# First eight chunks of w_mod: six of them split into high and low halves, and the gates of x taken before those of the context

## The chip, the cores and the metric

The kernel runs on one core of a Trainium2 chip. The metric is the device time of one execution in microseconds (us). The engines are TensorE (PE, with its weight loads as PEld), VectorE (DVE), ScalarE (ACT), GpSimd (POOL) and SyncE (SP), which issues most of the transfers. Each engine works through its own instructions in order; they meet only at semaphores.

## What is computed

Two transformer blocks in float32, on 256 tokens of width 1024. The change concerns the opening of the first block: the modulation vectors, the normalised and modulated x and context, and the forget gates of both.

```python
mod = (silu(c) @ w_mod[l] + b_mod[l]).reshape(bsz, 6, 1024)      # w_mod: 1024 x 6144
mc = (silu(c_ctx) @ w_mod[l] + b_mod[l]).reshape(6, 1024)
hc = modulate(rmsnorm(ctx, g_mix[l]), mc[0], mc[1])              # h * (1 + scale) + shift
pc = hc @ w_in[l][:, :1536]                                      # f_f, f_b (512 each), i_c (512)
h = modulate(rmsnorm(x, g_mix[l]), mod[:, 0, None], mod[:, 1, None])
p = h @ w_in[l]                                                  # f_f, f_b, i_in, q, og, u, v, ga, gb
f = lb + (1 - lb) * sigmoid(f_logit)                             # forget_gate; log(f) and 1 - f are used
```

All that follows (two linear recurrences started from the context's final state, a gating unit, five feed-forward parts, two attentions) is untouched by the change.

## The kernel before

Weights come as pieces of 128 x 1024 in the order of a list (`weight_plan`), through ten slots. For each piece `split` on ScalarE makes the high part WH (L991, a copy rounded to fp32r) and `split` on VectorE the low part WL = RAW - WH (L1485). A product then is three fp32r products (high by high, high by low, low by high), 128 x 128 by 256 columns each. SyncE loads piece j when the group that used piece j - 10 is done (`used`). In `split_to("win", i)` both engines split up to five pieces ahead of chunk i of w_in, and a chunk is two pieces.

Ahead of the list stand eight chunks of w_mod, `FIRST = (4, 5, 6, 7, 0, 1, 2, 3)` (chunks 0 to 3 are the shift, 4 to 7 the scale), 1 MB each, which lie in the memory of slots 0 to 7. They are used unsplit: `mod_first(i)` on TensorE makes float32 products of SILC (silu of c and c_ctx, two columns) with MC[i] (L442). The result is a pair of rows; VectorE copies it (`mod_rows(i)`, L1529), TensorE turns it into columns with four small products (`mods_finish`, L433), and VectorE adds the bias to give MOD (L1519, in its own `mods_finish`, run at the head of the next `mod_rows`). Chunks from 8 on come through the list, split, and are multiplied in `mods` (L456, L457) with SILH, which has high and low parts of the two vectors as four columns.

For the norms, ScalarE squares x (XF) and the context (XC) in eight steps (`square`, L1011), VectorE (x, "nx") or GpSimd (context, "nc") adds them up (`gather`), TensorE sums over the partitions (`sums`, L409), ScalarE takes the root (L1017), VectorE the reciprocal (`invert`, L1505), TensorE spreads it over the partitions (`spread`, L398) and ScalarE copies it to RB (`rows_kept`, L1024). Only then `modulated` can run: for each of eight k steps VectorE makes TA (L1550), ScalarE adds the shift and rounds to HH or, for the context, HCH (L1030), and VectorE makes the low part HL or HCL (L1559).

The gates are chunks 0 to 3 of w_in, for x (source 0) and for the context (source 1): 48 products a chunk and source, sigmoid on ScalarE into FX or FC (L1066), then lb + (1 - lb) f on VectorE (L1622). The order on TensorE is written out: chunks 0 and 1 of x, chunks 0 and 1 of the context, then chunk 2 of each, then chunk 3 of each, all with `by_k_step`, which for each k waits for that step's HL or HCL alone. `pair` is the other routine: it waits for what it is given once (here the eighth low part), then runs tile by tile. Chunks 4 and 5 of w_in (values, VTX and VTC) follow for both sources, then the queries, and the state work that starts with Ln of FC (L1083). The order of VectorE and ScalarE is written out too: the context's `modulated` stands behind the last of x and ahead of all gates. `rows_in(0)` is a 512 KB transfer (GROW) issued from ScalarE's queue, first used with chunk 8 of w_mod.

Of the kernel before, what the change touches and what calls it, by code (L numbers as in the profile page):

```python
# [12 lines left out]
P = 128  # L13
# [109 lines left out]
def build(nc, a, out):  # L123
# [3 lines left out]
    with ctx:  # L127
        base = [nc.sbuf_base]

        def at_(name, shape, off, dt=F32):  # L130
            return nc.alloc_sbuf_tensor_at(name, shape, dt, offset=off)
# [63 lines left out]
        MR = Ring([at_(f"MR{i}", [4, T], tmp_at + 9216 + 1024 * i) for i in range(2)])  # L195
        ROW = ph("ROW", 72, [P, 3, 512])
# [76 lines left out]
        RINGS = (RT, RS, RB, SQ, ACC, TA, MR, BANK, QK, AB, LNB, SPB, AW, SW, SX, PT, MX, SL, GG, Y, XN, TN)  # L273
# [65 lines left out]
        def pe_program(pe, e):  # L339
# [79 lines left out]
            def mods_finish():  # L419

                while rows:
                    i = rows.pop(0)
                    b, empty = bank(("modt", i), ("mod", i))
                    pe.wait_ge(*at("mr", i))
                    pe.wait_ge(*empty)
                    nr = 4 if i >= 8 else 2
                    mr = MR.of(("mr", i))
                    if i // 4 in (2, 5):
                        m = e.matmul(b[:, 0:T], CST[0:nr, C_SEL:C_SEL + 1].to_broadcast([nr, P]), mr[0:nr, :],
                                     start=True, stop=True)  # L430
                    else:
                        for t in range(2):
                            m = e.matmul(b[:, 2 * t:2 * t + 2], mr[0:nr, t * P:(t + 1) * P],  # L433
                                         CST[0:nr, C_SEL:C_SEL + 2], start=True, stop=True)
                    m.then_inc(*sig("modt", i))

            def mod_first(i):
                b, empty = bank(("modp", i), ("mr", i))
                pe.wait_ge(s_mod[i], 16)
                pe.wait_ge(*empty)  # L440
                for k in range(KD):
                    m = e.matmul(b[0:2, 0:T], SILC[:, 2 * k:2 * k + 2], MC[i][:, k * 256:k * 256 + 256],  # L442
                                 start=(k == 0), stop=(k == KD - 1))
                m.then_inc(*sig("modp", i))
                mods_finish()
                rows.append(i)
# [20 lines left out]
            mod_first(5)  # L467
            mod_first(6)
            sums("nx")
            mod_first(7)  # L470
            spread("nx")
            mod_first(0)
            mod_first(1)
            sums("nc")
            mod_first(2)
            spread("nc")
            mod_first(3)
# [3 lines left out]
            for c0, n in ((0, 2), (2, 1), (3, 1)):  # L481
                for src, (xh, xl, low) in enumerate(((HH, HL, "hl"), (HCH, HCL, "hcl"))):
                    group = [("win", c0 + z, ("fg", src, c0 + z), ("fs", src, c0 + z)) for z in range(n)]
                    for k in range(KD):
                        by_k_step(k, group, xh, xl, at(low, k))
# [496 lines left out]
        def act_program(ac, e):  # L982
# [58 lines left out]
            rows_in(0)  # L1041
            for k in range(KD):
                square("nx", k, XF[:, k, :], (s_xf, 16))
            root("nx")
            rows_kept("nx", ("hl", 7))
            for k in range(KD):
                square("nc", k, XC[:, k, :], (s_ctx, 16))
            modulated("h", 0, 0, HH, 0, 2, lambda k: at("mod", 0))
            root("nc")
            modulated("h", 0, 0, HH, 2, 4, lambda k: at("mod", 1))  # L1050
            rows_kept("nc", ("hcl", 7))
            split(1)
            modulated("h", 0, 0, HH, 4, 6, lambda k: at("mod", 2))
            split(3)
            modulated("h", 0, 0, HH, 6, 8, lambda k: at("mod", 3))
            modulated("hc", 0, 1, HCH, 0, 8, lambda k: at("mod", 3))
            ac.wait_ge(*at("dve", "lb", 1))
            e.activation(LBV[:, 8:24], LBV[:, 8:24], ACT.Exp).then_inc(*sig("act", "lb e"))
            split(5)


            for c0, n in ((0, 2), (2, 1), (3, 1)):
                for src, dst in enumerate((FX, FC)):
                    for c in range(c0, c0 + n):
                        ac.wait_ge(*at("fg", src, c))
                        e.activation(dst[:, 2 * c:2 * c + 2, :], two(BANK.of(("fg", src, c))[:, :]),  # L1066
                                     ACT.Sigmoid).then_inc(*sig("fs", src, c))
                split_to("win", c0 + n - 1)
# [407 lines left out]
        def dve_program(dv, e):  # L1476
# [46 lines left out]
            def mod_rows(i):  # L1523
                mods_finish()
                nr = 4 if i >= 8 else 2
                mr, before = MR.take(("mr", i), ("modt", i))
                dv.wait_ge(*at("modp", i))
                dv.wait_ge(*after(before))
                e.tensor_copy(mr[0:nr, :], BANK.of(("modp", i))[0:nr, 0:T]).then_inc(*sig("mr", i))  # L1529
                rows.append(i)  # L1530
# [39 lines left out]
            mod_rows(4)  # L1570
            for k in range(1, 7):
                gather("nx", k)
            mod_rows(5)
            mod_rows(6)
            invert("nx")
            mod_rows(7)
            mod_rows(0)
            dv.wait_ge(*at("mod", 7))
            scale_of("va", 0, S_GMIX, 8, 0)
            mod_rows(1)  # L1580
# [3 lines left out]
            invert("nc")  # L1584
            mod_rows(2)
            modulated("h", XF, RB.of(("rb", "nx")), 0, 0, 0, HH, HL, 2, 4)
            split(1)
            mod_rows(3)
            modulated("h", XF, RB.of(("rb", "nx")), 0, 0, 0, HH, HL, 4, 6)
# [4 lines left out]
            dv.wait_ge(*at("rb", "nc"))  # L1594
            dv.wait_ge(*at("dve", "vc"))
            modulated("hc", XC, RB.of(("rb", "nc")), 8, 0, 1, HCH, HCL, 0, 8)
# [15 lines left out]
            split(5)  # L1612


            dv.wait_ge(*at("dve", "lb", 5))
            for c0, n in ((0, 2), (2, 1), (3, 1)):
                for src, dst in enumerate((FX, FC)):
                    for c in range(c0, c0 + n):
                        dv.wait_ge(*at("fs", src, c))
                        for t in range(2):  # L1620
                            i = 2 * c + t
                            e.tensor_scalar(dst[:, i, :], dst[:, i, :], OMLB(i), LB(i), ALU.mult,  # L1622
                                            ALU.add).then_inc(*sig("fm", src, i))
                split_to("win", c0 + n - 1)
# [576 lines left out]
        def sp_program(sp, e):  # L2201
            e.dma_start(SM[:, :], a["small"]).then_inc(s_const, 16)
            e.dma_start(CST[:, :], a["cst"]).then_inc(s_const, 16)
            for z, i in enumerate(FIRST):
                if z == 1:
                    e.dma_start(XF[:, :, :], a["xf"]).then_inc(s_xf, 16)
                if z == 4:
                    e.dma_start(XC[:, :, :], a["ctx"]).then_inc(s_ctx, 16)
                e.dma_start(MC[i][:, :], a["mod"][i]).then_inc(s_mod[i], 16)
            for j, (kind, i, cols) in enumerate(plan):  # L2210
                if j >= SLOTS:
                    sp.wait_ge(*at(*used[j - SLOTS]))
                elif j >= 2:
                    sp.wait_ge(*at("modp", FIRST[j - 2]))
# [117 lines left out]
```

## Time and profile before

| | |
|---|---|
| median of three runs | 1638.43 us (1636.14 to 1641.19) |
| profiled execution | 1636.97 us, span 1635.7 us |
| busy, share of the span | PE 94%, DVE 56%, ACT 48%, POOL 3% |
| mean granted clock of TensorE | 0.962 of 2.4 GHz |
| moved | 267.11 MB, mean 163 GB/s |

The profile shows one execution. "Busy" of TensorE counts matmuls, which overlap, so that a product of 0.28 us may follow the one before it after 0.12. In rows of single instructions the bracket at the end gives the engine's idle time before them and what ended it. The chain of waits is followed back from the last instruction, at each step to what released it.

### The profile page before, as it was taken

The numbers are of one execution on the slowest core, as the hardware profiler recorded it, in microseconds if no ns is written. First come the engines' busy times: TensorE is split into PE (matmuls) and PEld (weight loads), VectorE is DVE, ScalarE is ACT, GpSimd is POOL, SyncE is SP. The second block draws the span as 40 slices with busy tenths as digits, with TensorE's granted clock in tenths as the row PEclk, the third lists the DMA queues.
The fourth block names the chain that finished last, engine by engine and source line by source line (L and its number), as shares of the span: only waits on it lengthen the run. The fifth ranks groups of instructions, "written<-read, shape, count | busy, mean of one in ns | idle before, by whom it ended". The sixth has DMA issues, their size and how long they took to land.

```text
span 1635.7 us, 20070 instructions
## 1 busy us (share of the span) xinstructions
PE 1540.1 (94%) x8188; PEld 1277.9 (78%) x8188; DVE 917.1 (56%) x1294; ACT 792.2 (48%) x1153; POOL 47.8 (3%) x83
## 2 busy tenths in 40 slices
PE   7998999998999999999999999999999777899998
PEld 3897888886888878887898788878888675578886
DVE  2627664877555565555455655556554457365553
ACT  2525435554445355544565555455554444365542
POOL 1000200000000000000021000000000011000000
PEclk9999788999999999999999999999999888799999
DMA  9225353644565655555533455555555410145652
GB/s 380 79 81 204 128 194 129 232 145 163 182 187 186 201 164 186 185 191 180 168 128 126 155 184 184 193 180 179 185 188 190 146 54 26 37 155 183 188 185 103
DMA packets 72236, 267.11 MB, mean 163 GB/s; under 512 B 8016, under 2 KB 8272, under 8 KB 70736
## 3 DMA queue, kind: packets, MB, share of 16 engines
q1 hardware_dynamic: 69984, 258.87, 48.0%
q10 hardware_dynamic: 2160, 6.95, 1.2%
q8 instruction: 65, 1.06, 0.3%
q14 instruction: 27, 0.22, 0.0%
HBM read 264.74 MB, written 1.05 MB: 162 GB/s over the span
## 4 chain that ended last, share of the span: by engine, by line
PE 83%; DVE 8%; ACT 5%; issue 2%; DMA 1%; POOL 0%; ACTq 0%; SPq 0%; DVEq 0%
PE PS L691 20%; PE PS L707 12%; PE PS L709 12%; PE PS L708 12%; PE PS L342 4%; PE PS L343 4%; PE PS L344 4%; DVE WL L1485 2%; ACT WH L991 2%; PE PS L675 1%; PE PS L442 1%; PE PS L374 1%; PE PS L375 1%; PE PS L376 1%; PE PS L563 1%
## 5 line engine op out<-in xcount | busy, mean ns | idle before, releaser
L1485 DVE TENSOR_TENSOR WL<-RAW,WH 128x1024 fp32r<-128x1024 f32 (+1 forms) x472 | 569.9, 1224 | 361.7 <-ACT WH L991 361.2
L991 ACT ACTIVATE WH<-RAW 128x1024 fp32r<-128x1024 f32 (+1 forms) x472 | 484.4, 1053 | 290.6 <-DMA RAW<-in_up 169.9
L707 PE MATMUL PS<-WH,XH 128*128 128x512 f32 x912 | 376.7, 413 | 24.5 <-DVE WL L1485 14.4
L709 PE MATMUL PS<-WH,XL 128*128 128x512 f32 x912 | 357.9, 392 | 0.0
L708 PE MATMUL PS<-WL,XH 128*128 128x512 f32 x912 | 357.7, 392 | 0.0
L707 PEld LDWEIGHTS PS<-WH,XH 128*128 128x128 f32 x912 | 172.2, 189 | 77.3 <-DVE WL L1485 18.3
L709 PEld LDWEIGHTS PS<-WH,XL 128*128 128x128 f32 x912 | 172.0, 189 | 37.0
L708 PEld LDWEIGHTS PS<-WL,XH 128*128 128x128 f32 x912 | 172.6, 189 | 27.7
L691 PE MATMUL PS<-WH,GH 128*128 128x512 f32 x440 | 137.3, 393 | 0.0
L691 PE MATMUL PS<-WL,GH 128*128 128x512 f32 x440 | 135.6, 389 | 0.0
L691 PE MATMUL PS<-WH,GL 128*128 128x512 f32 x440 | 135.6, 389 | 0.0
L691 PEld LDWEIGHTS PS<-WH,GL 128*128 128x128 f32 x440 | 82.6, 188 | 17.4
L691 PEld LDWEIGHTS PS<-WL,GH 128*128 128x128 f32 x440 | 82.6, 188 | 17.4
L691 PEld LDWEIGHTS PS<-WH,GH 128*128 128x128 f32 x440 | 81.2, 188 | 17.2
L1958 DVE SCALAR_TENSOR_TENSOR GG<-PS,RP,SL 128x256 f32<-128x256 f32 x88 | 42.6, 484 | 88.7 <-ACT SL L1291 88.7
L1298 ACT ACTIVATE GH<-PS 128x256 fp32r<-128x256 f32 x110 | 42.2, 384 | 90.9 <-PE PS L675 90.8
L342 PE MATMUL PS<-HH,WH 128*128 128x256 f32 x224 | 66.0, 295 | 0.0
L343 PE MATMUL PS<-HL,WH 128*128 128x256 f32 x224 | 65.3, 292 | 0.0
L344 PE MATMUL PS<-HH,WL 128*128 128x256 f32 x224 | 65.2, 291 | 0.0
L675 PE MATMUL PS<-CST,GG 128*128 128x128 f32 x220 | 58.8, 271 | 0.0
L1291 ACT ACTIVATE SL<-PS,RP 128x256 f32<-128x256 f32 x88 | 41.7, 474 | 28.7 <-PE PS L709 28.7
L342 PEld LDWEIGHTS PS<-HH,WH 128*128 128x128 f32 x224 | 45.1, 201 | 0.9 <-issue 0.3
(365 smaller groups left out, 2133.8 us busy)
## 6 DMA issues: line engine op xcount, KB each, us to landing
RAW<-in_up SPq DMA_DIRECT2D x220, 512.0 KB, 4.7
RAW<-in_down SPq DMA_DIRECT2D x110, 512.0 KB, 3.2
RAW<-in_win SPq DMA_DIRECT2D x44, 512.0 KB, 5.4
RAW<-in_mod SPq DMA_DIRECT2D x32, 512.0 KB, 4.9
MC<-in_mod SPq DMA_DIRECT2D x8, 1024.0 KB, 16.8
RAW<-in_sbqk SPq DMA_DIRECT2D x16, 512.0 KB, 4.8
GROW<-in_grow ACTq DMA_DIRECT2D x9, 512.0 KB, 4.6
RAW<-in_wo SPq DMA_DIRECT2D x8, 512.0 KB, 3.7
```

The lines of the kernel that those rows point to most:

```text
L342: e.matmul(out_, lh, rh, start=first, stop=False)
L343: e.matmul(out_, lh, rl, start=False, stop=False)
L344: return e.matmul(out_, ll, rh, start=False, stop=last)
L675: m = e.transpose(o_[:, y * P:(y + 1) * P], gg[:, y * P:(y + 1) * P], IDN)
L691: m = e.matmul(b2[n][:, :], l, r[:, n * 512:(n + 1) * 512], start=(first and z == 0), stop=(last and z == 2), skip_group_check=True)
L707: e.matmul(o_[:, :], l, w[:, s], start=(k == 0), stop=False, skip_group_check=True)
L708: e.matmul(o_[:, :], l, wl[:, s], start=False, stop=False, skip_group_check=True)
L709: m = e.matmul(o_[:, :], ll, w[:, s], start=False, stop=(k == KD - 1), skip_group_check=True)
L991: e.activation(WH[s][:, 0:c], RAW[s][:, 0:c], ACT.Copy).then_inc(*sig("hi", j))
L1298: e.activation(GH[:, 2 * j:2 * j + 2, h * P:(h + 1) * P], two(BANK.of(("gt", v, j, h))[:, 0:T]), ACT.Copy).then_inc(*sig("gh", v, j, h))
L1485: e.tensor_tensor(WL[s][:, 0:c], RAW[s][:, 0:c], WH[s][:, 0:c].bitcast(F32), ALU.subtract).then_inc(*sig("lo", j))
L1958: m = e.scalar_tensor_tensor(gg[:, :], u, RP[:, v, h:h + 1], sl[:, :], ALU.mult, ALU.mult)
```

## The change

Six of the eight chunks (`SPLIT`; not 4 and 6) are split like the others: ScalarE writes the high part of a chunk in two halves into a ring of two buffers MH_, VectorE writes the low part over the chunk in place (ML_), and the new `mod_split(i)` on TensorE multiplies SILH with both, k step by k step, waiting for each half. A high buffer comes free when the products of the chunk that used it are done. x is loaded ahead of the chunks, the context behind four pieces of w_in, GROW after the context's squares. The sums of x stand after the first chunk. The gates of x are taken for all four chunks (0 and 1 by k step, 2 and 3 with `pair`), with the context's sums and spread behind chunks 2 and 3; then the four chunks of the context, all with `pair`. ScalarE's squares and root of the context and VectorE's `invert`, `modulated` of the context move accordingly. `SPLIT` chunks have four rows instead of two in `mod_rows` and `mods_finish`.

```diff
@@ -193,6 +193,10 @@
+
+        SPLIT = (5, 7, 0, 1, 2, 3)
+        MH_ = Ring([ph(f"MCH{i}", 32 + 8 * i, [P, 2048], F32R) for i in range(2)])
+        ML_ = {i: at_(f"MCL{i}", [P, 2048], slot_at + 8192 * z, F32R) for z, i in enumerate(FIRST)}
...
@@ -423,7 +427,7 @@
-                    nr = 4 if i >= 8 else 2
@@ -441,6 +445,19 @@
+            def mod_split(i):
+
+                b, empty = bank(("modp", i), ("mr", i))
+                pe.wait_ge(*empty)
+                for k in range(KD):
+                    pe.wait_ge(*at("ml_", i, k // 4))
+                    c = slice(k * 256, k * 256 + 256)
+                    e.matmul(b[0:4, 0:T], SILH[:, k, :], MH_.of(("mh_", i))[:, c], start=(k == 0), stop=False)
+                    m = e.matmul(b[0:4, 0:T], SILH[:, k, :], ML_[i][:, c], start=False, stop=(k == KD - 1))
                 m.then_inc(*sig("modp", i))
                 mods_finish()
                 rows.append(i)
@@ -464,25 +481,28 @@
             pe.wait_ge(*CONST)
             pe.wait_ge(*at("dve", "silc low"))
             mod_first(4)
-            mod_first(5)
+            sums("nx")
+            mod_split(5)
             mod_first(6)
-            sums("nx")
-            mod_first(7)
             spread("nx")
-            mod_first(0)
-            mod_first(1)
+            for i in (7, 0, 1, 2, 3):
+                mod_split(i)
+            mods_finish()
+
+
+            def gates(src, c):
+                xh, xl, low = ((HH, HL, "hl"), (HCH, HCL, "hcl"))[src]
+                pair("win", c, ("fg", src, c), ("fs", src, c), xh, xl, at(low, 7))
+
+            group = [("win", c, ("fg", 0, c), ("fs", 0, c)) for c in range(2)]
+            for k in range(KD):
+                by_k_step(k, group, HH, HL, at("hl", k))
+            gates(0, 2)
             sums("nc")
-            mod_first(2)
+            gates(0, 3)
             spread("nc")
-            mod_first(3)
-            mods_finish()
-
-
-            for c0, n in ((0, 2), (2, 1), (3, 1)):
-                for src, (xh, xl, low) in enumerate(((HH, HL, "hl"), (HCH, HCL, "hcl"))):
-                    group = [("win", c0 + z, ("fg", src, c0 + z), ("fs", src, c0 + z)) for z in range(n)]
-                    for k in range(KD):
-                        by_k_step(k, group, xh, xl, at(low, k))
+            for c in range(4):
+                gates(1, c)
@@ -1038,34 +1058,55 @@
-            rows_in(0)
             for k in range(KD):
                 square("nx", k, XF[:, k, :], (s_xf, 16))
+
+            def mod_split(i):
+
+                mh, before = MH_.take(("mh_", i), ("modp", i))
+                ac.wait_ge(s_mod[i], 16)
+                ac.wait_ge(*after(before))
+                for z in range(2):
+                    c = slice(z * 1024, z * 1024 + 1024)
+                    e.activation(mh[:, c], MC[i][:, c], ACT.Copy).then_inc(*sig("mh_", i, z))
+
+            mod_split(5)
             root("nx")
+            mod_split(7)
             rows_kept("nx", ("hl", 7))
+            for i in (0, 1, 2, 3):
+                mod_split(i)
+                if i == 2:
+                    modulated("h", 0, 0, HH, 0, 2, lambda k: at("mod", 0))
+            split(0)
+            modulated("h", 0, 0, HH, 2, 4, lambda k: at("mod", 1))
+            split(3)
+            modulated("h", 0, 0, HH, 4, 6, lambda k: at("mod", 2))
+            modulated("h", 0, 0, HH, 6, 8, lambda k: at("mod", 3))
+            split(5)
             for k in range(KD):
                 square("nc", k, XC[:, k, :], (s_ctx, 16))
-            modulated("h", 0, 0, HH, 0, 2, lambda k: at("mod", 0))
-            root("nc")
-            modulated("h", 0, 0, HH, 2, 4, lambda k: at("mod", 1))
-            rows_kept("nc", ("hcl", 7))
-            split(1)
-            modulated("h", 0, 0, HH, 4, 6, lambda k: at("mod", 2))
-            split(3)
-            modulated("h", 0, 0, HH, 6, 8, lambda k: at("mod", 3))
-            modulated("hc", 0, 1, HCH, 0, 8, lambda k: at("mod", 3))
+            rows_in(0)
             ac.wait_ge(*at("dve", "lb", 1))
             e.activation(LBV[:, 8:24], LBV[:, 8:24], ACT.Exp).then_inc(*sig("act", "lb e"))
-            split(5)
-
-
-            for c0, n in ((0, 2), (2, 1), (3, 1)):
-                for src, dst in enumerate((FX, FC)):
-                    for c in range(c0, c0 + n):
-                        ac.wait_ge(*at("fg", src, c))
-                        e.activation(dst[:, 2 * c:2 * c + 2, :], two(BANK.of(("fg", src, c))[:, :]),
-                                     ACT.Sigmoid).then_inc(*sig("fs", src, c))
-                split_to("win", c0 + n - 1)
+            split(7)
+
+
+            def gates(src, c):
+                ac.wait_ge(*at("fg", src, c))
+                e.activation((FX, FC)[src][:, 2 * c:2 * c + 2, :], two(BANK.of(("fg", src, c))[:, :]),
+                             ACT.Sigmoid).then_inc(*sig("fs", src, c))
+
+            gates(0, 0)
+            gates(0, 1)
+            root("nc")
+            gates(0, 2)
+            rows_kept("nc", ("hcl", 7))
+            gates(0, 3)
+            modulated("hc", 0, 1, HCH, 0, 8, lambda k: at("mod", 3))
+            for c in range(4):
+                gates(1, c)
+                split_to("win", c)
@@ -1567,33 +1608,45 @@
-            mod_rows(4)
+            def mod_split(i):
+
+                for z in range(2):
+                    c = slice(z * 1024, z * 1024 + 1024)
+                    dv.wait_ge(*at("mh_", i, z))
+                    e.tensor_tensor(ML_[i][:, c], MC[i][:, c], MH_.of(("mh_", i))[:, c].bitcast(F32),
+                                    ALU.subtract).then_inc(*sig("ml_", i, z))
+
             for k in range(1, 7):
                 gather("nx", k)
+            mod_split(5)
+            mod_rows(4)
             mod_rows(5)
+            mod_split(7)
             mod_rows(6)
             invert("nx")
+            mod_split(0)
             mod_rows(7)
+            mod_split(1)
             mod_rows(0)
             dv.wait_ge(*at("mod", 7))
             scale_of("va", 0, S_GMIX, 8, 0)
+            mod_split(2)
             mod_rows(1)
             dv.wait_ge(*at("rb", "nx"))
             dv.wait_ge(*at("dve", "va"))
             modulated("h", XF, RB.of(("rb", "nx")), 0, 0, 0, HH, HL, 0, 2)
-            invert("nc")
+            mod_split(3)
+            split(0)
             mod_rows(2)
             modulated("h", XF, RB.of(("rb", "nx")), 0, 0, 0, HH, HL, 2, 4)
-            split(1)
             mod_rows(3)
+            split(2)
             modulated("h", XF, RB.of(("rb", "nx")), 0, 0, 0, HH, HL, 4, 6)
             mods_finish()
             split(3)
             modulated("h", XF, RB.of(("rb", "nx")), 0, 0, 0, HH, HL, 6, 8)
             scale_of("vc", 8, S_GMIX, 8, 1)
-            dv.wait_ge(*at("rb", "nc"))
-            dv.wait_ge(*at("dve", "vc"))
-            modulated("hc", XC, RB.of(("rb", "nc")), 8, 0, 1, HCH, HCL, 0, 8)
+            split(5)
@@ -1609,19 +1662,27 @@
-            split(5)
-
-
+            split(7)
+
+
+            def gates(src, c):
+                dv.wait_ge(*at("fs", src, c))
+                dst = (FX, FC)[src]
+                for t in range(2):
+                    i = 2 * c + t
+                    e.tensor_scalar(dst[:, i, :], dst[:, i, :], OMLB(i), LB(i), ALU.mult,
+                                    ALU.add).then_inc(*sig("fm", src, i))
+
+            invert("nc")
+            dv.wait_ge(*at("rb", "nc"))
+            dv.wait_ge(*at("dve", "vc"))
+            modulated("hc", XC, RB.of(("rb", "nc")), 8, 0, 1, HCH, HCL, 0, 8)
             dv.wait_ge(*at("dve", "lb", 5))
-            for c0, n in ((0, 2), (2, 1), (3, 1)):
-                for src, dst in enumerate((FX, FC)):
-                    for c in range(c0, c0 + n):
-                        dv.wait_ge(*at("fs", src, c))
-                        for t in range(2):
-                            i = 2 * c + t
-                            e.tensor_scalar(dst[:, i, :], dst[:, i, :], OMLB(i), LB(i), ALU.mult,
-                                            ALU.add).then_inc(*sig("fm", src, i))
-                split_to("win", c0 + n - 1)
+            for c in range(4):
+                gates(0, c)
+            for c in range(4):
+                gates(1, c)
+                split_to("win", c)
@@ -2201,13 +2262,12 @@
         def sp_program(sp, e):
             e.dma_start(SM[:, :], a["small"]).then_inc(s_const, 16)
             e.dma_start(CST[:, :], a["cst"]).then_inc(s_const, 16)
-            for z, i in enumerate(FIRST):
-                if z == 1:
-                    e.dma_start(XF[:, :, :], a["xf"]).then_inc(s_xf, 16)
-                if z == 4:
-                    e.dma_start(XC[:, :, :], a["ctx"]).then_inc(s_ctx, 16)
+            e.dma_start(XF[:, :, :], a["xf"]).then_inc(s_xf, 16)
+            for i in FIRST:
                 e.dma_start(MC[i][:, :], a["mod"][i]).then_inc(s_mod[i], 16)
             for j, (kind, i, cols) in enumerate(plan):
+                if j == 4:
+                    e.dma_start(XC[:, :, :], a["ctx"]).then_inc(s_ctx, 16)
                 if j >= SLOTS:
                     sp.wait_ge(*at(*used[j - SLOTS]))
                 elif j >= 2:
```

## Rows read from the trace of the kernel before

**Rows 1.** Page, chain that ended last: share of the span by engine

```profile
PE 83%; DVE 8%; ACT 5%; issue 2%; DMA 1%; POOL 0%; ACTq 0%; SPq 0%; DVEq 0%
```

**Rows 2.** Stretches: length, busy PE PEld DVE ACT POOL, clock, DMA share, GB/s

```profile
10.00:20.00 10.00, 8.65 (x41) 3.43 (x40) 3.35 (x9) 2.62 (x8) 0.00 (x0) 1.00 1.01 412
...
60.00:70.00 10.00, 10.00 (x86) 10.00 (x85) 5.91 (x16) 6.27 (x8) 0.00 (x0) 1.00 0.01 2
```

**Rows 3.** Timeline of TensorE, first two chunks: start, length, instruction, idle time before

```profile
7.21 5.14 PE L442 MATMUL PS<-MC,SILC 128*2 128x256 f32 x16 [7.21 <-DMA MC<-in_mod]
...
13.71 3.62 PE L442 MATMUL PS<-MC,SILC 128*2 128x256 f32 x16 [1.35 <-DMA MC<-in_mod]
```

**Rows 4.** Chain of waits, opening: start, length, engine and line

```profile
26.99 0.64 PE PS L398 x4
...
35.25 0.53 PE PS L433 x4
35.78 0.98 PE PS L409 x8
36.77 3.54 PE PS L442 x16
...
43.94 2.36 DVE WL L1485 x2
...
47.12 0.91 ACT HH L1030 x2
...
50.87 0.21 PE PS L375
```

**Rows 5.** Timeline, gates: first product with HCH, last sigmoid of FC

```profile
63.10 0.28 PE L374 MATMUL PS<-HCH,WH 128*128 128x256 f32 x1
...
97.86 0.60 ACT L1066 ACTIVATE FC<-PS 128x512 f32<-128x512 f32 x1 [5.16 <-PE PS L376]
```

**Rows 6.** Timeline of TensorE, transposes after the values

```profile
136.93 3.46 PE L502 MATMUL PS<-CST,Pc 128*128 128x128 f32 x16 [4.55 <-DVE Pc L1641]
```

**Rows 7.** Timeline of TensorE, first and seventeenth product of the split chunk 8

```profile
155.31 0.28 PE L456 MATMUL PS<-WH,SILH 128*4 128x256 f32 x1
...
157.15 0.28 PE L456 MATMUL PS<-WH,SILH 128*4 128x256 f32 x1
```

**Rows 8.** Groups of instructions, 0 to 50 us: count, busy us, mean ns, idle

```profile
L991 ACT ACTIVATE WH<-RAW 128x1024 fp32r<-128x1024 f32 x4 | 4.0, 1042 | 0.0
L1529 DVE COPY MR<-PS 2x256 f32<-2x256 f32 x8 | 3.2, 402 | 6.1 <-PE PS L442 6.1
...
L1541 DVE TENSOR_TENSOR VEC<-VEC,SM 128x8 f32<-128x8 f32 x1 | 0.6, 626 | 0.0
```

**Rows 9.** Timeline: RB of x, GpSimd's sums, context's vectors, a table load

```profile
27.66 0.39 ACT L1024 ACTIVATE RB<-PS 128x256 f32<-128x256 f32 x1 [4.45 <-PE PS L398]
28.74 5.07 POOL L2168 TENSOR_TENSOR ACC<-ACC,SQ 128x256 f32<-128x256 f32 x6 [28.23 <-ACT SQ L1011]
...
53.60 0.88 DVE L1550 SCALAR_TENSOR_TENSOR TA<-XC,VEC,RB 128x256 f32<-128x256 f32 x2
60.83 0.49 DVE L1559 SCALAR_TENSOR_TENSOR HCL<-TA,MOD,HCH 128x256 fp32r<-128x256 f32 x1 [0.18 <-ACT HCH L1030]
...
60.81 1.28 ACT L1058 ACT_TABLE_LOAD   x1
```

**Rows 10.** Stretches of 1 us around two dips of the clock (columns of rows 2)

```profile
48.00:49.00 1.00, 0.45 (x3) 0.16 (x1) 0.62 (x3) 1.00 (x3) 0.00 (x0) 0.50 0.06 25
...
54.00:55.00 1.00, 1.00 (x8) 1.00 (x7) 0.82 (x3) 0.88 (x2) 0.00 (x0) 0.65 0.00 0
...
137.00:138.00 1.00, 1.00 (x5) 1.00 (x6) 1.00 (x1) 1.00 (x2) 0.00 (x0) 0.50 0.31 123
...
140.00:141.00 1.00, 1.00 (x10) 1.00 (x9) 0.98 (x2) 1.00 (x2) 0.00 (x0) 0.98 0.00 0
```

**Rows 11.** Timeline of TensorE, recurrence outputs ahead of and in the slow stretch

```profile
186.09 0.43 PE L563 MATMUL PS<-QI,S 128*128 128x64 f32 x2
...
189.16 0.69 PE L561 MATMUL PS<-SC,VTX 64*128 64x64 f32 x2
```

More of the change, by code:

```diff
@@ L272, in build @@
         KD_ = at_("KD_", [P, 4, T], x_at + 12288)
-        RINGS = (RT, RS, RB, SQ, ACC, TA, MR, BANK, QK, AB, LNB, SPB, AW, SW, SX, PT, MX, SL, GG, Y, XN, TN)
+        RINGS = (RT, RS, RB, SQ, ACC, TA, MR, MH_, BANK, QK, AB, LNB, SPB, AW, SW, SX, PT, MX, SL, GG, Y, XN, TN)
         R4 = slice(64, 96)
@@ L425, in mods_finish @@
                     pe.wait_ge(*empty)
-                    nr = 4 if i >= 8 else 2
+                    nr = 4 if i >= 8 or i in SPLIT else 2
                     mr = MR.of(("mr", i))
@@ L443, in mod_first @@
                                  start=(k == 0), stop=(k == KD - 1))
+                m.then_inc(*sig("modp", i))
+                mods_finish()
+                rows.append(i)
+            def mod_split(i):
[6 more added lines that the diff above has]
+                    m = e.matmul(b[0:4, 0:T], SILH[:, k, :], ML_[i][:, c], start=False, stop=(k == KD - 1))
                 m.then_inc(*sig("modp", i))
@@ L466, in pe_program @@
             mod_first(4)
-            mod_first(5)
+            sums("nx")
+            mod_split(5)
             mod_first(6)
-            sums("nx")
-            mod_first(7)
             spread("nx")
-            mod_first(0)
-            mod_first(1)
+            for i in (7, 0, 1, 2, 3):
+                mod_split(i)
+            mods_finish()
+            def gates(src, c):
[5 more added lines that the diff above has]
+            gates(0, 2)
             sums("nc")
-            mod_first(2)
+            gates(0, 3)
             spread("nc")
-            mod_first(3)
-            mods_finish()
-            for c0, n in ((0, 2), (2, 1), (3, 1)):
-                for src, (xh, xl, low) in enumerate(((HH, HL, "hl"), (HCH, HCL, "hcl"))):
-                    group = [("win", c0 + z, ("fg", src, c0 + z), ("fs", src, c0 + z)) for z in range(n)]
-                    for k in range(KD):
-                        by_k_step(k, group, xh, xl, at(low, k))
+            for c in range(4):
+                gates(1, c)
             for c in range(2):
@@ L1524, in mod_rows @@
                 mods_finish()
-                nr = 4 if i >= 8 else 2
+                nr = 4 if i >= 8 or i in SPLIT else 2
                 mr, before = MR.take(("mr", i), ("modt", i))
```

## The prediction

> **What bounds the kernel now.** I read the page first: the chain that ended last is TensorE for 83% of its length [rows 1]. That is a mean; the change touches only the opening, so the table of stretches comes next [rows 2]. Until 40 us the DMA share is 1.0 at some 410 GB/s while VectorE and ScalarE are mostly idle; from 60 to 120 us TensorE is full at full clock and the other two have room; only 40 to 60 us is mixed. The timeline shows which wait ends last. TensorE takes the first chunk of w_mod at 7.21, waits for the second until 13.71, and then has its own work as the bound: 3.54 us a chunk in the chain, so that the seventh is begun only at 36.77, when its data has long landed [rows 3, 4]. Then the chain crosses to VectorE and ScalarE (modulated x, splits of w_in) until 50.3; from there product follows product [rows 4]. TensorE goes through: the two first gate chunks of x end at 63.10, where the first product with HCH stands, and the last of the other six groups at 97.7, where the last sigmoid of FC follows [rows 5], 5.76 us a group. I call 63.1 point A and 97.7 point E.
>
> What follows E hangs on E alone. The value chunks run until 120.8, then the chain goes over ScalarE's copy of VTC, Ln, scans and Exp to the transposes at 136.93, for which TensorE idles 4.55 us [rows 6]. That idle time is no cover for the change: its chain starts with TensorE's own product, so it moves with E. The loads of this stretch wait for slots that TensorE frees; the new order frees the slots of w_in chunks 0, 1 and 2 later against E (17.3, 11.5 and 5.8 us before it instead of 23.0, 23.0 and 11.5), yet their successors, chunks 5 to 7, are wanted 11.5 us after E or later, and a load lands in some 5 us. The loads don't become late. So the question is by how much E moves.
>
> **Part by part, up to A.** (1) *Loads.* x goes ahead of all chunks, GROW (0.5 MB) leaves the opening, the context (1 MB) goes behind four pieces of w_in. At 412 GB/s a chunk of 1.05 MB takes 2.55 us [rows 2]. The first transfer landed at 7.2, so x does, chunk 4 at 9.7 (2.5 later for TensorE's first work), chunk 5 at 12.4 and the others at 2.6 us steps, chunk 3 at 28.3. (2) *Products.* An unsplit chunk takes 3.54 us [rows 4]. The same shape with split weights exists later: 16 products from 155.31 to 157.15, 1.84 us [rows 7]. Six chunks save 6 x 1.70 = 10.2 us of TensorE. (3) *Splits.* Each of the six costs VectorE 2.36 us for its two halves of 1024 columns [rows 4] and ScalarE 1.99 (1.04 for one [rows 8], the second a little overlapped), that is 14.2 and 12 us on engines that were idle there. But each also puts VectorE between the chunks, in program order, ahead of the row copies on which the next products wait.
>
> Worked through in program order with these prices, and with 0.48 us for the add of one chunk and the row copy of the next (0.40 the copy), 0.53 for four small products, and 1.9 for a modulated pair (0.44 the first on VectorE, 0.91 both on ScalarE, 0.49 the last low) [rows 4, 8, 9]: the first chunk runs on TensorE from 9.7 to 14.8 (5.14 us, as its first chunk took in [rows 3]); sums of x to 15.8; the splits of chunk 5 end at 16.0, its products at 17.7, chunk 6 unsplit from 18.2 to 21.8. VectorE copies the row of 6 at 22.8 and only then inverts, so TensorE waits 0.8 us and the spread of x ends at 23.7. ScalarE has queued the copy of RB before the split of chunk 0, so that split starts at 24.1. From here VectorE is last at every step: lows of chunk 0 to 27.5, row copy 28.0, chunk 1 to 30.4, row, scale 31.25, chunk 2 to 33.6, row 34.1, modulated pair 36.0, chunk 3 to 38.9 (ScalarE begins its half at 35.5, behind the pair), w_in piece 0 to 40.1, row 40.6, pair 42.5, row 43.0, pieces 1 and 2 to 45.4. At 45.4 TensorE has the second chunk of the first k step; later pairs (47.3, 50.5) and piece 3 (48.6) are ready before their steps. 0.72 + 7 x 1.44 us gives A = 56.2 at full clock.
>
> The clock is the unknown. In the trace the granted clock fell to 0.50, the 1.2 GHz level, at 48, after TensorE had been idle or nearly so from 45.5, and came back within 54 to 55: products at a pitch of 0.21 [rows 4] instead of 0.12, some 20 of them, 1.9 us lost. After the 4.55 us idle it fell within 136 to 137 and was back at 140, 1.5 us lost [rows 10]. In the new opening TensorE is busy a bit more than half of the time from 27 to 43, with holes near 36 and 39. I take 1.4 us (bounds 0 and 1.9): A = 57.6, which is 5.5 us earlier than 63.1.
>
> **From A to E.** Before, E - A was 6 x 5.76 = 34.6, with the context's vectors made on VectorE beside the gates of x (53.60 to 61.32, 7.72 us for eight k steps at a pitch of 0.92) [rows 9]. Now TensorE does chunk 2, the sums of the context (0.98), chunk 3, and then the spread (0.64) [rows 4]: 5.76 x 2 + 1.62 = 13.1, so the spread ends at 70.7. Only from it can ScalarE copy RB (0.39 us in [rows 9] for x, plus some 0.1 of hand-over), and only then VectorE starts on XC: 7.72 us, and 0.1 since ScalarE's sigmoid of chunk 3 stands ahead of the first bias. The gates of the context are no longer taken k by k: the pair routine waits for the eighth HCL before its first product. **TensorE is idle for 0.5 + 7.72 + 0.1 = 8.3 us**, 70.7 to 79.0. The old order had the same 7.72 us hidden under the products of x; the new one has no work on TensorE left to hide it. The clock then falls again: 1.8 us (bounds 0 and 2.1, the nearest row being the dip at 137). E = 79.0 + 4 x 5.76 + 1.8 = 103.8.
>
> Costed at nothing: the rest of the work moved. The ctx squares with GpSimd's sums (5.07 us) now stand behind w_in piece 5 on ScalarE, from 52 to 58 [rows 9]; then Exp and pieces 6 and 7, done by 62.2, wanted at 64.3: 2 us of cover. If GpSimd's sums hold VectorE back (an operation of VectorE on 8 columns took 626 ns beside them, more than the copy of 256 [rows 8]) that cover shrinks, at most by a few such. Root of the context now lies between sigmoids, which costs two more table loads of 1.28 us [rows 9] on ScalarE; they end by 67 and the next thing wanted there is at 70.7. The Trainium skill, ScalarE: Activation LUTs, What ACT_TABLE_LOAD costs, gives about 2.66 us for a switch with its drain, and its section Table sets advises to group activations by set, which speaks against this order; by its figure the second switch would end near 70, still before the spread, and the sum would stay.
>
> **Sum.** 103.8 - 97.7 = +6.1 us: minus 5.5 up to A, plus 13.1 + 8.3 + 24.8 - 34.6 = +11.6 behind it. The profiled execution took 1636.97 us (span 1635.7); the median of three runs is 1638.43, 1.5 above it. I give the time against the median: 1644.5.
>
> **The rivals.** (a) *The clock stays up.* If neither hole costs the clock anything, 3.2 us go from the sum: +2.9, 1641.3; with one of the two, +4.3 to +4.7. For: the 1.35 us wait at 12.4 to 13.7 cost nothing [rows 3]. Against: 8.3 us idle is nearly twice the idle time that lowered it at 137. The Trainium skill, TensorE: Matmul & The Clock Gate, Part 1, says that when the clock changes depends on a phase that differs from run to run; no single trace shows that, and by it the losses could lie anywhere between my bounds. (b) *TensorE at 1.2 GHz already between 27 and 43.* Then products and small products of chunks 7 to 3 take twice as long (3.7 and 1.1 us), a split waits for the products two chunks back (the ring MH_ has two buffers), and the chain goes over TensorE and ScalarE instead of VectorE: 1 to 1.6 us more at chunks 7, 1 and 2, some 4 us in all: +10, 1648.5. It decides from the point where the clock falls before 30 us. For: half-busy TensorE. Against: until 23.7 it is nearly full. (c) *Not slower.* Behind E lies a stretch at 1.2 GHz: from 187.9 to 208.2 the products of L561 and L563 go at 0.62 us a pair of rows instead of 0.36 [rows 11]. 26 such pairs x 0.25 and 20 products x 0.10 are 8.5 us. If the shifted phase keeps the clock up there, the sum is 6.1 - 8.5 = -2.4, 1636.0, and with (a) -5.6. For: the fall came only 2 us into that work. Against: what TensorE does before it is the same in both kernels.
>
> **How the numbers follow.** A measurement of this kernel can tell about 0.3%, 4.9 us, from no change. Forecast (+4.9 to +8): 0.50. (a) +2.5 to +4.9: 0.27. (b) +8 to +12: 0.14. (c): 0.09, of which 0.05 below -4.9 and 0.04 within. Slower 0.64, same 0.31, faster 0.05. The range takes in (a) down to +2 and (b) up to +12, and leaves out (c): 1640 to 1651.
>
> **What would show it.** TensorE's idle time before the first product with HCH: 8.3 us, released by VectorE's HCL. That product at 79, the first sigmoid of FC after 84.7, the last group of the context done at 103.8. First 96 products of x done at 57.6. The new split products: 1.84 us a chunk. VectorE busy without a break from 25 to 50. Behind E every distance as before. I'd be wrong if the gate products of the context began within 2 us of the spread, if A came before 53, or if the stretch after E changed its length.

## The result and the profile after

The changed kernel takes 1646.39 us in the median of six runs (1644.77 to 1648.08), the kernel before 1638.81 (1636.14 to 1641.19): 7.6 us more, a ratio of 1.0047 with a 95% interval of 1.0034 to 1.006. The profiled execution took 1648.08 us.

| | before | after |
|---|---|---|
| median | 1638.81 us | 1646.39 us |
| span of the profiled execution | 1635.7 us | 1646.5 us |
| first 96 products of x done (A) | 63.1 us | 57.9 us |
| TensorE idle ahead of the context's gates | none | 8.22 us |
| last sigmoid of FC starts (0.15 behind E) | 97.86 us | 104.29 us |
| VTC copied | 120.90 us | 127.33 us |

The page of the changed kernel, span and the chain that ended last, says little: as in [rows 1], TensorE is the chain for 83%, with 1% more of VectorE.

```profile
span 1646.5 us, 20098 instructions
...
PE 83%; DVE 9%; ACT 5%; issue 2%; DMA 0%; POOL 0%; ACTq 0%; SPq 0%; DVEq 0%
```

The timeline of the changed kernel's opening (start, length, engine, instruction; in brackets the idle time before and its releaser) answers to [rows 3] and [rows 7]:

```profile
9.77 6.17 PE L446 MATMUL PS<-MC,SILC 128*2 128x256 f32 x16 [9.77 <-DMA MC<-in_mod]
12.13 2.00 ACT L1071 ACTIVATE MCH<-MC 128x1024 fp32r<-128x1024 f32 x2 [1.52 <-DMA MC<-in_mod]
13.22 2.36 DVE L1616 TENSOR_TENSOR MCL<-MC,MCH 128x1024 fp32r<-128x1024 f32 x2 [2.00 <-ACT MCH L1071]
...
16.79 0.28 PE L459 MATMUL PS<-MCH,SILH 128*4 128x256 f32 x1
...
18.54 0.28 PE L460 MATMUL PS<-MCL,SILH 128*4 128x256 f32 x1
...
24.81 0.38 ACT L1044 ACTIVATE RB<-PS 128x256 f32<-128x256 f32 x1 [5.68 <-PE PS L402]
...
26.18 2.36 DVE L1616 TENSOR_TENSOR MCL<-MC,MCH 128x1024 fp32r<-128x1024 f32 x2 [2.17 <-ACT MCH L1071]
...
38.13 0.28 PE L459 MATMUL PS<-MCH,SILH 128*4 128x256 f32 x1 [2.32 <-DVE MCL L1616]
...
43.05 2.36 DVE L1526 TENSOR_TENSOR WL<-RAW,WH 128x1024 fp32r<-128x1024 f32 x2
...
57.95 0.28 PE L346 MATMUL PS<-HH,WH 128*128 128x256 f32 x1
```

The sixteen split products of chunk 5 begin at 16.79 and the last at 18.54, so a chunk takes 1.87 us with the last one's share, against 3.54 unsplit. The rows at 24.81 and 26.18 show why TensorE's shorter work isn't the whole story: VectorE stands idle 2.17 us because ScalarE copies RB first and splits chunk 0 after it. At 38.13 TensorE itself has waited 2.32 us for VectorE. At 45.41 (43.05 + 2.36) the second piece of w_in is split, and the first product of chunk 2 of x, at 57.95, is point A.

The same view around the gates answers to [rows 5], [rows 6] and [rows 9]:

```profile
71.00 0.38 ACT L1044 ACTIVATE RB<-PS 128x256 f32<-128x256 f32 x1 [4.13 <-PE PS L402]
...
71.42 0.88 DVE L1591 SCALAR_TENSOR_TENSOR TA<-XC,VEC,RB 128x256 f32<-128x256 f32 x2 [6.26 <-ACT RB L1044]
...
78.64 0.48 DVE L1600 SCALAR_TENSOR_TENSOR HCL<-TA,MOD,HCH 128x256 fp32r<-128x256 f32 x1 [0.18 <-ACT HCH L1050]
79.18 0.58 PE L346 MATMUL PS<-HCH,WH 128*128 128x256 f32 x1 [8.22 <-DVE HCL L1600]
...
87.01 0.60 ACT L1097 ACTIVATE FC<-PS 128x512 f32<-128x512 f32 x1 [8.40 <-PE PS L348]
...
104.29 0.60 ACT L1097 ACTIVATE FC<-PS 128x512 f32<-128x512 f32 x1 [3.27 <-PE PS L348]
...
127.33 0.60 ACT L1113 ACTIVATE VTC<-PS 128x512 f32<-128x512 f32 x1 [5.16 <-PE PS L348]
```

VectorE waited 6.26 us for RB, then made the eight steps of the context in 7.7 us while TensorE stood for 8.22. The spread that releases RB ended at 70.96 (79.18 - 8.22), 13.0 us behind A. From FC's last sigmoid to VTC's copy there are 23.04 us in both kernels (120.90 - 97.86 before): up to there the work behind E moves along as a block.

Stretches of the changed kernel (length, busy PE PEld DVE ACT POOL, granted clock, DMA share, GB/s) answer to [rows 10]:

```profile
36.00:38.00 2.00, 0.00 (x0) 0.00 (x0) 1.54 (x3) 2.00 (x3) 0.00 (x0) 1.00 1.02 408
38.00:40.00 2.00, 1.87 (x12) 1.07 (x13) 2.00 (x3) 0.72 (x1) 0.00 (x0) 0.72 1.02 410
...
48.00:50.00 2.00, 2.00 (x14) 2.00 (x14) 1.82 (x5) 1.09 (x3) 0.00 (x0) 0.72 0.00 0
...
72.00:74.00 2.00, 0.00 (x0) 0.00 (x0) 1.75 (x5) 1.33 (x3) 0.00 (x0) 0.75 0.00 0
...
80.00:82.00 2.00, 2.00 (x11) 2.00 (x11) 1.72 (x6) 0.00 (x0) 0.00 (x0) 0.50 0.00 0
82.00:84.00 2.00, 2.00 (x14) 2.00 (x14) 0.00 (x0) 0.00 (x0) 0.00 (x0) 0.69 0.00 0
```

Both dips came: the first just after TensorE's wait of 2.32 us, when it was at work again (1.00 until 38, 0.72 from 38 to 40), lasting until between 48 and 50, the second from between 72 and 74 until between 82 and 84, four of its ten microseconds under work.

### The profile page after: what moved, and what is told of

Its sections match the earlier page's. It is cut to its first block, busy times and chain, and to the rows that moved or that the text cites. A ratio compares the mean times of both kernels' runs of the same rounds, so it can differ in the third digit from the quotient of the medians.

```text
span 1646.5 us, 20098 instructions
## 1 busy us (share of the span) xinstructions
PE 1540.3 (94%) x8188; PEld 1284.5 (78%) x8188; DVE 931.7 (57%) x1306; ACT 805.8 (49%) x1167; POOL 42.6 (3%) x83
## 4 chain that ended last, share of the span: by engine, by line
PE 83%; DVE 9%; ACT 5%; issue 2%; DMA 0%; POOL 0%; ACTq 0%; SPq 0%; DVEq 0%
PE PS L711 21%; PE PS L727 12%; PE PS L729 12%; PE PS L728 12%; PE PS L346 4%; PE PS L347 4%; PE PS L348 4%; DVE WL L1526 2%; ACT WH L1011 2%; PE PS L695 1%; PE PS L583 1%; PE PS L581 1%; DVE TN L1963 1%; PE PS L473 1%; PE PS L474 1%
## 5 line engine op out<-in xcount | busy, mean ns | idle before, releaser
L346 PE MATMUL PS<-HH,WH 128*128 128x256 f32 x256 | 75.4, 294 | 0.0
L347 PE MATMUL PS<-HL,WH 128*128 128x256 f32 x256 | 74.6, 291 | 0.0
L348 PE MATMUL PS<-HH,WL 128*128 128x256 f32 x256 | 74.4, 291 | 0.0
L346 PEld LDWEIGHTS PS<-HH,WH 128*128 128x128 f32 x256 | 51.5, 201 | 1.2 <-DVE WL L1526 0.7
```

Source lines behind the costliest of these rows:

```text
L346: e.matmul(out_, lh, rh, start=first, stop=False)
L347: e.matmul(out_, lh, rl, start=False, stop=False)
L348: return e.matmul(out_, ll, rh, start=False, stop=last)
```

## The experiments

Theory 1 is that of the prediction: the opening gains some 5 us, and the wait for the context's vectors with its dip loses more. Theory 2: the loss lies behind the gates, since the changed kernel's profile is 4.4 us longer there (1542.2 us from FC's last sigmoid to the end, 1537.8 before). "The sigmoid" below is FC's last. Ratios are against the kernel before on the same chip, in five rounds; its median was 1638.81, 1639.24 and 1639.33 us in the three sets of runs, so medians of different sets can be compared to about 0.5 us.

**The spread one chunk earlier, and k by k.**

```diff
+            sums("nc")
             gates(0, 2)
-            sums("nc")
-            gates(0, 3)
             spread("nc")
-            for c in range(4):
-                gates(1, c)
+            gates(0, 3)
+            group = [("win", c, ("fg", 1, c), ("fs", 1, c)) for c in range(2)]
+            for k in range(KD):
+                by_k_step(k, group, HCH, HCL, at("hcl", k))
+            for c in range(2, 4):
+                gates(1, c)
```

> The changed kernel with two edits on TensorE alone: the context's sums stand ahead of chunk 2 of x and its spread ahead of chunk 3 (each one chunk earlier), and chunks 0 and 1 of the context are taken k by k instead of waiting for the eighth low part. Theory 1 (the loss is TensorE's wait for the context's vectors, 8.2 us in the changed kernel's profile, and the clock dip behind it): the spread then ends near 65, VectorE is three k steps into the context when chunk 3 of x ends at 71.1, the wait is gone, the four chunks of the context take 23.0 us, and the last of them ends at 94 instead of 104. That is 10 us less than the changed kernel and 3.6 less than the kernel before, 1635. Theory 2 (the loss lies behind the gates, where the changed kernel's profile is 4.4 us longer than that of before, by the clock falling elsewhere): the wait goes all the same, but at most 3 us of the total with it, 1643 or more.

Measured: 1638.22 us (ratio 0.9997, 0.9988 to 1.0006), 8.2 us less than the changed kernel, 3 more than theory 1 had it. The timeline of this kernel says why:

```profile
66.07 0.38 ACT L1047 ACTIVATE RB<-PS 128x256 f32<-128x256 f32 x1
71.36 0.60 ACT L1100 ACTIVATE FX<-PS 128x512 f32<-128x512 f32 x1 [4.91 <-PE PS L348]
...
72.93 0.39 PE L378 MATMUL PS<-HCH,WH 128*128 128x256 f32 x1 [1.60 <-DVE HCL L1603]
...
96.26 0.60 ACT L1100 ACTIVATE FC<-PS 128x512 f32<-128x512 f32 x1 [3.27 <-PE PS L348]
```

RB was there at 66.1, but on ScalarE the sigmoid of chunk 3 of x stands ahead of the context's first pass and waited for TensorE until 71.36. So moving the spread brought next to nothing by itself: TensorE still waited 1.60 us, against 2.06 in the next kernel, which leaves the spread where it was. What was expected of the spread was wrong; that the wait is the loss was right.

**K by k alone.**

```diff
-            for c in range(4):
-                gates(1, c)
+            group = [("win", c, ("fg", 1, c), ("fs", 1, c)) for c in range(2)]
+            for k in range(KD):
+                by_k_step(k, group, HCH, HCL, at("hcl", k))
+            for c in range(2, 4):
+                gates(1, c)
```

> The changed kernel with one edit: chunks 0 and 1 of the context are taken k by k, the spread stays behind chunk 3 of x. It tells how much of the wait is the late spread and how much the change from k by k to all at once. Theory 1: the first low part is there some 1.6 us after VectorE starts on the context (71.4), so TensorE starts at 73.0 instead of 79.2; a k step of two chunks (1.44 us) is longer than one of VectorE (0.92), so no further wait; the clock still falls for a few us. The last chunk ends at 98, 6 us less than the changed kernel, about the time of before: 1640. Rival: a low clock comes anyway with the same full length, and TensorE starting earlier at 1.2 GHz wins only half, 1643.

Measured: 1639.80 us (ratio 1.0002, 0.9993 to 1.0012), the time that was expected. Its timeline:

```profile
70.01 0.38 ACT L1047 ACTIVATE RB<-PS 128x256 f32<-128x256 f32 x1 [4.13 <-PE PS L402]
...
72.03 0.38 PE L378 MATMUL PS<-HCH,WH 128*128 128x256 f32 x1 [2.06 <-DVE HCL L1603]
...
95.36 0.60 ACT L1100 ACTIVATE FC<-PS 128x512 f32<-128x512 f32 x1 [3.27 <-PE PS L348]
```

One edit on TensorE takes the wait from 8.22 to 2.06 us and 6.6 us off the median. From 72.03 to the sigmoid there are 23.3 us, full speed: after 2.06 us idle the clock did not fall here (in the opening it did fall behind 2.32 us), so this dip goes with the long wait, and the rival is out. The agreement of the time is partly luck, though: with the dip gone and the opening 1.0 us earlier the sigmoid came at 95.36, nearly 3 us ahead of what was expected, while the median fell by 6.6 us only.

**All chunks unsplit.**

```diff
-        SPLIT = (5, 7, 0, 1, 2, 3)
+        SPLIT = ()
```

(with `mod_first` in place of `mod_split` on TensorE, and no chunk's splits on ScalarE and VectorE)

> The changed kernel with all eight chunks unsplit (SPLIT empty): the order of loads, gates and context stays. It gives what the splits alone bring. Theory 1: TensorE is then the bound of the opening: 9.8 to 15.8, sums, seven chunks of 4.07 us with their small products and the spread, the last product at 44.9, rows of chunk 3 at 45.4, pieces 1 and 2 of w_in split by 47.8, first 96 products of x done near 60 (changed kernel 57.9). So the splits bring 2 to 2.5 us only, not the 10.2 us that they take from TensorE: 1649. Rival (splits bring what TensorE's products get shorter): 10 us more than the changed kernel, 1656.

Measured: 1651.67 us (ratio 1.0076, 1.0063 to 1.0088), 5.3 more than the changed kernel; the sigmoid at 108.28, 4.0 later. Timeline of TensorE and ScalarE:

```profile
9.74 6.38 PE L446 MATMUL PS<-MC,SILC 128*2 128x256 f32 x16 [9.74 <-DMA MC<-in_mod]
...
42.85 3.62 PE L446 MATMUL PS<-MC,SILC 128*2 128x256 f32 x16
...
47.57 0.60 PE L437 MATMUL PS<-CST,MR 2*128 2x2 f32 x4 [0.57 <-DVE MR L1565]
...
83.31 0.58 PE L346 MATMUL PS<-HCH,WH 128*128 128x256 f32 x1 [8.22 <-DVE HCL L1595]
...
108.28 0.60 ACT L1092 ACTIVATE FC<-PS 128x512 f32<-128x512 f32 x1 [3.27 <-PE PS L348]
```

The splits bring 4 to 5 us, of 10 us that they take from TensorE; the rest VectorE takes back. I had expected 2.5: the unsplit opening ends 1.5 us later than worked out (last product 46.4, not 44.9), 1.2 of it in the first chunk, 6.38 us long instead of 5.14. Point A is at 62.1 here, so of the 5.2 us by which A moved, 4.1 are the splits and 1.0 the order of loads and sums. And the wait of 8.22 us stands here as well: it comes from the order of the gates, not from the splits.

**The split opening with the old order of gates.** TensorE's gates are those of before, k by k for both sources in turn; the context's vectors are made early:

```diff
             for i in (7, 0, 1, 2, 3):
                 mod_split(i)
+            sums("nc")
             mods_finish()
...
+                        by_k_step(k, group, xh, xl, at(low, k))
+                        if c0 == 0 and src == 0 and k == 1:
+                            spread("nc")
```

> The split opening with the gate order of before: chunks 0 and 1 of x, then of the context, then chunk 2 and chunk 3 of each, all k by k; for this the context is loaded ahead of the last chunk of w_mod, its squares stand in two fours behind the splits of chunks 2 and of piece 0, its sums behind the last split product, its spread behind the second k step of x, its vectors behind piece 5 on VectorE. Theory 1: the opening's gain stays whole (first 96 products of x done at 58 to 59 with the spread among them) and nothing is lost behind it: the last chunk of the context ends near 93.7, 4 us ahead of before: 1635. Theory 2 (the loss is behind the gates): the stretch behind stays 4 us longer as in the changed kernel, 1639.

Measured: 1638.54 us (ratio 0.999, 0.9981 to 0.9999), between the theories. Its timeline has RB of the context and the sigmoid at

```profile
51.55 0.39 ACT L1039 ACTIVATE RB<-PS 128x256 f32<-128x256 f32 x1 [0.33 <-PE PS L402]
...
94.73 0.60 ACT L1100 ACTIVATE FC<-PS 128x512 f32<-128x512 f32 x1 [5.16 <-PE PS L380]
```

The opening did nearly as theory 1 has it: the sigmoid comes 3.1 us ahead of [rows 5] (4 expected). But this profile took 1543.5 us behind it, and of the 3.1 us the median gives back 0.7 and the ratio 1.6. That left theory 2 open for the stretch behind E, and the last two runs below are for it.

**ScalarE's order mended.**

```diff
             rows_kept("nc", ("hcl", 7))
-            gates(0, 3)
             modulated("hc", 0, 1, HCH, 0, 8, lambda k: at("mod", 3))
+            gates(0, 3)
```

> The kernel with the early spread (e1) and one more edit: on ScalarE the first pass over the context's vectors stands ahead of the sigmoid of chunk 3 of x, not behind it. In e1 ScalarE had copied RB at 66.1 and then stood at that sigmoid until 71.4, so that the context's vectors began no earlier than with the late spread. Theory: now they begin at 66.5, TensorE goes from chunk 3 of x straight into the context at 71.4, and the last sigmoid of FC starts at 94.6 (e1 96.3, changed kernel 104.3): 1636.7, that is 1.6 less than e1 and 2.5 less than the kernel before. Rival: what stands behind the gates takes longer by as much in the new orders; then there is no gain over e1, 1638.

Measured: 1635.59 us (ratio 0.9981, 0.9971 to 0.999), 2.6 less than the kernel with the early spread, and ahead of the kernel before by 3.7 by the medians, 3.1 by the ratio.

```profile
65.05 0.38 ACT L1047 ACTIVATE RB<-PS 128x256 f32<-128x256 f32 x1
72.56 0.58 ACT L1100 ACTIVATE FX<-PS 128x512 f32<-128x512 f32 x1
...
93.79 0.60 ACT L1100 ACTIVATE FC<-PS 128x512 f32<-128x512 f32 x1 [3.27 <-PE PS L348]
```

The sigmoid of chunk 3 of x now stands behind the context's vectors and costs nobody anything; TensorE has no wait left in this stretch, and FC's last sigmoid is 10.5 us ahead of the changed kernel's. Of the 2.5 us against the kernel with the early spread 1.60 are that kernel's wait; in this profile the spread also ended 0.6 earlier, which the edit doesn't explain.

**Less on VectorE.** Five chunks split instead of six, and chunk 0 split ahead of RB's copy:

```diff
-        SPLIT = (5, 7, 0, 1, 2, 3)
+        SPLIT = (5, 7, 0, 1, 2)
...
             mod_split(7)
+            mod_split(0)
             rows_kept("nx", ("hl", 7))
```

> e5 with less on VectorE's path in the opening: the split of chunk 0 stands ahead of the copy of RB on ScalarE (VectorE stood idle 2.2 us for it), and chunk 3 is left unsplit (2.4 us less of VectorE, 1.7 more of TensorE, which has room there). Theory (VectorE is last at every step from 24 to 45): first 96 products of x done near 53 instead of 57.9, the last sigmoid of FC starts near 90: 4.5 us less than e5, 1632, ahead of the kernel before by 0.4%. Rival (TensorE's products are what lasts in the opening): 1.7 us more than e5, 1638.

Measured: 1631.39 us (ratio 0.9949, 0.9935 to 0.9964), the fastest version: 7.9 us ahead of before, 15 ahead of the changed kernel. Its timeline (the low part of chunk 0, the sigmoid):

```profile
22.73 2.33 DVE L1620 TENSOR_TENSOR MCL<-MC,MCH 128x1024 fp32r<-128x1024 f32 x2
...
90.50 0.60 ACT L1101 ACTIVATE FC<-PS 128x512 f32<-128x512 f32 x1 [3.27 <-PE PS L348]
```

VectorE goes into chunk 0 without waiting, and the two edits together took 3.3 us at the sigmoid (93.79 to 90.50) and 4.2 in the median, although TensorE works 1.7 us longer on chunk 3. So TensorE's products were not the bound of the opening; VectorE's path was. The first 96 products of x were done at 54.4, not 53. How the gain divides between the two edits, and how much of it is ScalarE's share of the split (2.0 us), wasn't measured.

**Both kernels once more, for the stretch behind E.**

> The kernel before, unchanged, for a second profile. If the length of the stretch from the last sigmoid of FC to the end depends on when the clock happens to fall, it differs from the 1537.8 us of the first profile by some us (the other five kernels had 1540.3 to 1543.5 with the same work); if it is the change that makes it longer, it is 1538 again.

> The changed kernel, unchanged, for a second profile: last sigmoid of FC at 104.3 within 1.5 us (the dips of the clock move), and the stretch behind it anywhere from 1538 to 1543 if the clock's dips decide it, 1542 if the change does.

Measured: 1641.93 and 1647.24 us. The kernel before, second time, had a span of 1640.6 us, the sigmoid at 97.29 and so 1543.3 us behind it, 5.5 more than in its first profile. The changed kernel repeated its wait and had the sigmoid at 103.62, with 1542.2 us behind it:

```profile
78.58 0.58 PE L346 MATMUL PS<-HCH,WH 128*128 128x256 f32 x1 [8.22 <-DVE HCL L1600]
...
103.62 0.60 ACT L1097 ACTIVATE FC<-PS 128x512 f32<-128x512 f32 x1 [3.27 <-PE PS L348]
```

Nearly half of what the kernel before differs from itself shows in one stretch, VTC's copy to the first product with SC. First profile:

```profile
120.90:185.70 64.80, 57.47 (x472) 52.84 (x470) 52.24 (x74) 37.13 (x44) 8.85 (x2) 0.95 0.56 195
```

second profile:

```profile
120.30:187.60 67.30, 60.34 (x472) 55.37 (x471) 52.53 (x74) 37.13 (x44) 2.94 (x2) 0.90 0.55 188
```

The same 472 products, 74 operations of VectorE and 44 of ScalarE take 2.5 us longer at a mean granted clock of 0.90 instead of 0.95. The rest of the 5.5 us comes bit by bit: FC's sigmoid was 0.57 us earlier than in the first profile, and ScalarE's table loads start 1.9 us later at 268, 4.0 at 524 and 4.95 at 1582. All ten profiles together have 1537.8 to 1543.5 us behind the sigmoid, the kernel before at both ends but for 0.2 us. A fairer measure is the median span of all runs of a kernel less the sigmoid of its profiles (the mean of both where there are two): 1540.4 us for the kernel before and 1541.0 for the changed kernel. Of the 4.4 us 0.6 are left, and theory 2 falls: the rest was the first profile of before, which happened to have high clock.

## Why the prediction was right

The sum was +6.1 us and the time 1644.5; measured were +7.6 (5.6 to 9.8 by the interval) and 1646.39. E moved by 6.4 us in the first pair of profiles and 6.3 in the second, and what is left lies behind E, within the scatter.

- *Up to A: right.* Forecast 57.6, measured 57.9. The prices of the parts held (split products 1.87 us a chunk against 1.84, splits 2.36 and 2.00). The first chunk was mis-sized: 6.17 us instead of 5.14. That it did no harm is luck: the lows of chunk 0 were done at 28.54 instead of 27.5, but the steps behind it took a little less each than their prices, and the second piece of w_in was split at 45.41, forecast 45.4. From there the dip cost 1.7 us, not 1.4. "VectorE busy without a break from 25" was too strong: it idled until 26.18 and 0.46 us more at 36.4, for ScalarE's split of chunk 3. That VectorE's path and not TensorE's products is the bound there is shown by the unsplit kernel (splits bring 4 to 5 us, not 10) and by the last version, which is faster with one split less and an earlier start of VectorE.
- *The wait: right.* 8.3 forecast, 8.22 in both profiles, from 70.96 to 79.18, released by HCL. The runs split it: 6.2 us are the change from k by k to all at once, and 1.6 to 2.1 are the place of the context's first pass, which took two moves, TensorE's spread and ScalarE's sigmoid. The prediction gave the sigmoid 0.1 us, which is right in the changed kernel; I overlooked that it would be the next bound as soon as the spread is moved.
- *The clock: right.* 1.8 us forecast behind the wait; 104.29 - 79.18 - 23.04 = 2.1, less some 0.15 from the last product to the sigmoid, is 1.9. Without the long wait (k by k) there was no loss. The dip in the opening began at 38 to 40, so rival (b), a fall before 30, didn't happen, nor did (a).
- *What was costed at nothing cost nothing.* In the changed kernel pieces 6 and 7 of w_in were split by 61.8 (forecast 62.2, wanted 64.3); the table loads ended at 66.3. By the Trainium skill's figure for a switch (ScalarE: Activation LUTs, What ACT_TABLE_LOAD costs; about 2.66 us with its drain) the prediction's estimate for their end was near 70. Here the trace disagrees; timeline of ScalarE in the changed kernel:

```profile
62.73 1.28 ACT L1037 ACT_TABLE_LOAD   x1
64.70 0.26 ACT L1037 ACTIVATE VEC<-PS,VEC 128x2 f32<-128x2 f32 x1 [0.69 <-PE PS L413]
64.98 1.28 ACT L1097 ACT_TABLE_LOAD   x1
66.28 0.60 ACT L1097 ACTIVATE FX<-PS 128x512 f32<-128x512 f32 x1
```

  The first load ran ahead of the wait for the sums, and the sigmoid started 0.02 us behind the second: 1.28 us each, no drain.
- *Rival (c), the slow stretch of the recurrence outputs:* it went at low clock in all profiles. One sign of being wrong, a changed length of the stretch after E, seemed to be there, 4.4 us in the first pair of profiles; by the medians it is 0.6. But the clock does decide some 5 us behind E from run to run, and that is what makes the measured 7.6 uncertain by 2. Whether an order changes the mean length of the stretch behind E by a microsecond or two stays open: by median span less sigmoid it is 1539.6 to 1543.1 us in the six kernels of the experiments, longest in the one with k by k alone (1543.1) and the one with the old gate order (1542.6), and these rest on one profile each for the sigmoid.

## What to carry to other kernels

When work is reordered so that one engine gets longer unbroken runs, look at what the other engines had been doing under the work that is moved: here 7.7 us of VectorE's steps were hidden under the gates of x, and the new order put their trigger, the spread, behind the last work that could hide them. A routine that waits for all of an operand is as good as one that waits step by step only while the operand has long been there. A wait has to be removed on every engine in its chain: the spread on TensorE was moved for nothing while ScalarE's queue kept a sigmoid ahead of it. And what is taken from the bounding engine should be weighed against the engine that pays for it: six splits took 10 us from TensorE and brought 4 to 5.

## What the runs showed of the hardware

The clock's dips move from run to run in the same program. In the changed kernel's wait of 8.22 us the clock fell 2 us after TensorE went idle in one profile and some 5 us after it in the other; stretches of the first and the second profile:

```profile
73.00:74.00 1.00, 0.00 (x0) 0.00 (x0) 0.96 (x3) 0.48 (x1) 0.00 (x0) 0.51 0.00 0
...
75.00:76.00 1.00, 0.00 (x0) 0.00 (x0) 0.96 (x3) 0.59 (x2) 0.00 (x0) 0.83 0.00 0
```

Where two profiles of the kernel before were compared, the stretch behind E was 1537.8 us in one and 1543.3 in the other, the part looked at with more time at the low clock in the second; a difference of 4 us between two single profiles was no finding.

TensorE's first chunk of float32 products took from 5.00 to 6.38 us in the ten profiles, although the granted clock is shown as 1.00 there in the changed kernel and in the unsplit one (6.17 and 6.38 us); later chunks took 3.54. No run shows why.
